# Two transformer blocks on one core: the three products of branches and output as seven quarter products each

## What is computed

```python
a = gmlp_spatial_gating(z_u, z_v, gmlp_ln_g[i], gmlp_ln_b[i], gmlp_w_s[i], gmlp_b_s[i])
b = forgetting_attention(q, k, v, f_logit, b_f[i])
y_a = jnp.einsum('bsc,cd->bsd', a, w_branch_a[i])
y_b = jnp.einsum('bsc,cd->bsd', b, w_branch_b[i])
merged = gate_a * y_a + gate_b * y_b
x = x + jnp.einsum('bsd,de->bse', merged, w_out[i])
h2 = rmsnorm_2(x, norm_ffn_g[i])
up = jnp.einsum('bsd,df->bsf', h2, w_up[i])
```

## Time and profile before

| | us |
|---|---|
| median of 3 runs (1606.82 to 1606.89) | 1606.87 |
| profiled execution, its own time | 1607.59 |
| its span on the core | 1605.9 |
| TensorE busy | 1587.6 (99%) |
| VectorE busy | 1078.5 (67%) |
| ScalarE busy | 710.6 (44%) |
| POOL busy | 181.5 (11%) |

### The profile page before, as it was taken

One profiled execution on the slowest core, in us unless ns is written; L12 is line 12 of the kernel. 1 busy time (PEld: TensorE's weight loads), 2 busy tenths in 40 slices (PEclk: granted clock), 3 DMA queues, 4 the chain that ended last, 5 costly groups with the idle time before them and its releaser, 6 DMA issues.

```text
span 1605.9 us, 20446 instructions
## 1 busy us (share of the span) xinstructions
PE 1587.6 (99%) x8187; PEld 1305.8 (81%) x8187; DVE 1078.5 (67%) x1494; ACT 710.6 (44%) x1018; POOL 181.5 (11%) x263
## 2 busy tenths in 40 slices
PE   9999999999999999999999999999999999999998
PEld 7877777888888888878788887888888888888888
DVE  6756788669393865657744477445566876878857
ACT  6524575545252524415662156342334443443544
POOL 0001055000000000024500255000000000000000
PEclk9999999999999999999999999999999999999999
DMA  5233321264757522331022211322237347344221
GB/s 191 80 106 125 123 95 53 79 210 131 236 132 235 131 106 94 116 138 72 27 105 83 101 53 53 136 101 105 93 143 262 102 135 238 93 154 158 105 106 53
DMA packets 32894, 195.14 MB, mean 122 GB/s; under 512 B 4320, under 2 KB 6816, under 8 KB 11296
## 3 DMA queue, kind: packets, MB, share of 16 engines
q1 hardware_dynamic: 25056, 160.20, 27.0%
q0 software_dynamic: 2880, 20.97, 6.8%
q10 hardware_dynamic: 4864, 12.66, 2.2%
HBM read 187.50 MB, written 6.32 MB: 121 GB/s over the span
## 4 chain that ended last, share of the span: by engine, by line
PE 87%; DVE 7%; issue 2%; ACT 2%; POOL 1%; DMA 0%; DVEq 0%; ACTq 0%; POOLq 0%
PE bank L767 20%; PE bank L769 19%; PE bank L768 19%; PE bank L1189 3%; PE bank L1190 3%; PE bank L1191 3%; PE bank L815 3%; PE bank L817 3%; PE bank L816 3%; PE bank L1000 1%; PE bank L775 1%; PE bank L985 1%; DVE w_lo L2370 1%; PE bank L744 1%; DVE up_c L2668 1%
## 5 line engine op out<-in xcount | busy, mean ns | idle before, releaser
L767 PE MATMUL bank<-a_hi,w_hi 128*128 128x512 f32 x1160 | 456.8, 394 | 0.6 <-DVE x L2030 0.6
L769 PE MATMUL bank<-a_hi,w_lo 128*128 128x512 f32 x1160 | 452.0, 390 | 0.0
L768 PE MATMUL bank<-a_lo,w_hi 128*128 128x512 f32 x1160 | 451.6, 389 | 0.0
L1375 ACT ACTIVATE w_hi<-w_raw 128x2048 fp32r<-128x2048 f32 x95 | 181.3, 1908 | 184.5 <-DMA w_raw<-in_strips 182.7
L769 PEld LDWEIGHTS bank<-a_hi,w_lo 128*128 128x128 f32 x1160 | 217.8, 188 | 45.9
L767 PEld LDWEIGHTS bank<-a_hi,w_hi 128*128 128x128 f32 x1160 | 217.9, 188 | 45.3 <-issue 2.3
L768 PEld LDWEIGHTS bank<-a_lo,w_hi 128*128 128x128 f32 x1160 | 218.0, 188 | 43.0 <-issue 0.2
L1951 DVE TENSOR_TENSOR w_lo<-w_raw,w_hi 128x2048 fp32r<-128x2048 f32 x92 | 210.9, 2293 | 54.4 <-ACT w_hi L1375 54.3
L1189 PE MATMUL bank<-w_hi,t_hi 128*128 128x512 f32 x280 | 109.3, 390 | 0.1
L1191 PE MATMUL bank<-w_hi,t_lo 128*128 128x512 f32 x280 | 109.0, 389 | 0.0
L1190 PE MATMUL bank<-w_lo,t_hi 128*128 128x512 f32 x280 | 109.0, 389 | 0.0
(11 more groups left out here) (364 smaller groups left out, 2658.0 us busy)
## 6 DMA issues: line engine op xcount, KB each, us to landing
w_raw<-in_strips SPq DMA_DIRECT2D x107, 1024.0 KB, 4.8
a_part<-in_parts SPq DMA_DIRECT2D x25, 1024.0 KB, 7.4
a_part<-in_parts POOLq DMA_DIRECT2D x20, 1024.0 KB, 9.1
spare<-in_parts SPq DMA_DIRECT2D x5, 1024.0 KB, 15.0
spare<-in_strips SPq DMA_DIRECT2D x5, 1024.0 KB, 4.9
seg_in<-cum_kept ACTq DMA_DIRECT2D x16, 256.0 KB, 3.5
x_kept<-x ACTq DMA_DIRECT2D x2, 2048.0 KB, 9.2
x<-x_kept SPq DMA_DIRECT2D x2, 2048.0 KB, 9.9
```

What stands on the lines that cost most here:

```text
L767: mm(ps[:, :], w_hi[slot][:, k, cols], hi[:, k, :], start=(k == 0), stop=False)
L768: mm(ps[:, :], w_hi[slot][:, k, cols], lo[:, k, :], start=False, stop=False)
L769: return mm(ps[:, :], w_lo[slot][:, k, cols], hi[:, k, :], start=False, stop=(k == kt - 1))
L1375: run(w_hi[j], w_raw[j], ACT.Copy).then_inc(hi_split, 1)
```

## The change

branch_b, branch_a and out2 are each computed as seven products of quarters. The weight (1024 x 1024) is cut in four quarters of 512 x 512, the operand in four of 512 features x 256 positions (`quad(buf, i, j)`: position half i, feature half j). Each product has one weight quarter or a sum of quarters as stationary operand, 48 matmuls of 256 columns into two banks, of which each holds two feature tiles. Products 2 and 3 add onto the banks of products 0 and 1, product 4 onto those of product 2.

- **Weights.** Four of the seven weights per matrix are sums (of 2, 2, 3 and 4 quarters). They are made in DRAM ahead of time: SP copies a quarter to `pre` behind each of twelve strip loads from ff2_3 on, and POOL issues twelve DMAs that add to them, six in attention 2a, one per head, and six during u and qk2b. In the new stages the strips are loaded to buffers of their own, two in turn (`fold_raw`, in the place of `x` for the branches, elsewhere for out2), each after VectorE has split the strip before the last.
- **Operands.** Four quarters (`high_four`, `low_four`: three plain, one a difference) and three further sums (`high_three`, `low_three`) per stage; VectorE makes the sums (`fold_sums`), partly over the operand itself. Those of branch_b are begun in gate_a, those of branch_a in branch_b, and those of out2 as soon as a quarter of `merged` is there.
- **Results.** ScalarE keeps the first two products' banks in SBUF (`keep_first`, `keep_second`), VectorE combines (`keep_sums`, `take_11`, `take_21`, `take_22`, `take_12`, `gate_part`, `add_known`). GpSimd does none of this work.
- **x** is read back in two halves in branch_a, with SP waiting for strips' splits, and the tiles' norm for up0 is done in two groups of four. The first weight parts of down0 are loaded after out2's last read of a bank.

The diff, cut to its core:

```diff
 PHASES += [(f"{w}{g}", 7 if f"{w}{g}" in SEVEN else 4) for g in range(FF_GROUPS) for w in ("ff1_", "ff2_")]
...
+FOLD_BANK = [6, 4, 6, 4, 6, 0, 2]
+FOLD_QUAD = [1, 0, 1, 2, 3, 0, 2]
+FOLD_FOUR = {0: 1, 1: 0, 3: 2, 4: 3}
+FOLD_THREE = {2: 0, 5: 1, 6: 2}
+THREE_QUAD = [(1, 0), (0, 0), (0, 1)]
+THREE_RAW = [(0, 0), (1, 0), (0, 1)]
+FOLD_SOURCE = [0, (0, 0), 2, (1, 0), 3, 1, (1, 1)]
+PRE_SUMS = [(0, 1), (0, 0), (0, 0), (1, 0)]
+PRE_COPIES = [(kind, f) for kind in range(4) for f in range(3)]
...
+                    sp_eng.wait_ge(dve_evac, EVAC0["out2"] + FILLS["out2"])
...
+                if s in FOLDED:
+                    n = s - FIRST[FOLD[0]]
+                    if n == 0:
+                        sp_eng.wait_ge(pv_done, 2 * 3 * HEADS8)
+                        sp_eng.wait_ge(summed, 16 * (12 + 4 * FF_SEVEN))
+                    elif n == 14:
+                        sp_eng.wait_ge(fold_step, FOLD_STEP0 + 5)
+                    elif n == 15:
+                        sp_eng.wait_ge(*low_ready(s - 3))
+                    elif n != 1:
+                        sp_eng.wait_ge(*low_ready(s - 2))
+                    f, i = FOLDED[s]
+                    source = FOLD_SOURCE[i]
+                    sp_eng.dma_start(flat(fold_at(s)), pre[source, f] if isinstance(source, int) else fold_part(f, source)).then_inc(fold_loaded[n % 3], 16)
+                    if n == 15:
+                        for h in range(2):
+                            sp_eng.wait_ge(*low_ready(s - 3 + h))
+                            half = slice(4 * h, 4 * h + 4)
+                            sp_eng.dma_start(x[:, half, :], x_kept[:, half, :]).then_inc(x_loaded[0], 16)
+                    continue
...
+                if 0 <= s - FIRST["ff2_3"] - 1 < len(PRE_COPIES):
+                    kind, f = PRE_COPIES[s - FIRST["ff2_3"] - 1]
+                    sp_eng.dma_start(pre[kind, f], fold_part(f, PRE_SUMS[kind])).then_inc(copied[kind // 2], 16)
...
-                if s == FIRST["gate_a"] + 3:
-                    sp_eng.wait_ge(pv_done, 2 * 3 * HEADS8)
-                    sp_eng.dma_start(x, x_kept).then_inc(x_loaded[0], 16)
...
+                    if call == "2a" and n % TT == 2 and 1 <= n // TT <= 6:
+                        add_part(*PRE_COPIES[n // TT - 1])
...
+            def add_part(kind, f):
+                if f == 0:
+                    pool.wait_ge(summed, 16 * (4 * FF_SEVEN + (0, 0, 6, 9)[kind]))
+                if f == 0 and kind in (0, 2):
+                    pool.wait_ge(copied[kind // 2], COPIED0[kind // 2] + 16 * 6)
+                other = (fold_part(f, (1, 1)), fold_part(f, (0, 1)), pre[0, f], pre[2, f])[kind]
+                pool.dma_start(pre[kind, f], other, accum_op=ALU.add, max_dma_last_dim=8192).then_inc(summed, 16)
...
+            for n, (kind, f) in enumerate(PRE_COPIES[6:]):
+                pool.wait_ge(unit_done, 2 * (FIRST["u"] + n + 1))
+                add_part(kind, f)
...
-            stream("branch_b", feature_k, B, ready=lambda k: pe.wait_ge(att_lo, 4 + k + 1))
-            stream("branch_a", feature_k, A, ready=wait_tiles(amix_lo))
-            stream("out2", feature_k, B, ready=wait_tiles(m_lo))
...
+            def folded(f):
+                for i in range(7):
+                    s = FIRST[FOLD[f]] + i
+                    slot, (t, k0) = s % W_SLOTS, QUADS[FOLD_QUAD[i]]
+                    hi, lo = quad(fold_hi[f], t, k0), quad(fold_lo[f], t, k0)
+                    pe.wait_ge(*low_ready(s))
+                    if i in FOLD_THREE:
+                        pe.wait_ge(three_lo, 3 * f + FOLD_THREE[i] + 1)
+                    else:
+                        pe.wait_ge(four_lo, 4 * f + FOLD_FOUR[i] + 1)
+                    for h in range(2):
+                        fold_bank(f, i, h)
+                        for e in range(2):
+                            ps = bank[FOLD_BANK[i] + h][:, e * (T // 2):(e + 1) * (T // 2)]
+                            cols = slice((2 * h + e) * P, (2 * h + e + 1) * P)
+                            for k in range(W4):
+                                mm(ps, w_hi4[slot][:, k, cols], hi[:, k, :], start=(e == 0 and k == 0 and i in (0, 1, 5, 6)), stop=False, skip_group_check=True)
+                                mm(ps, w_hi4[slot][:, k, cols], lo[:, k, :], start=False, stop=False, skip_group_check=True)
+                                last = mm(ps, w_lo4[slot][:, k, cols], hi[:, k, :], start=False, stop=(k == W4 - 1), skip_group_check=True)
+                        last.then_inc(unit_done, 1)
...
+            def high_strip(f, i):
+                s = FIRST[FOLD[f]] + i
+                act.wait_ge(fold_loaded[(s - FIRST[FOLD[0]]) % 3], fold_count(s))
+                act.wait_ge(unit_done, 2 * (s - W_SLOTS) + 2)
+                run(w_hi[s % W_SLOTS], fold_at(s), ACT.Copy).then_inc(hi_split, 1)
...
+            def high_three(f, n):
+                act.wait_ge(fold_sum, FOLD_SUM0 + 4 * f + (3, 2, 4)[n])
+                act.wait_ge(unit_done, 2 * (FIRST[FOLD[f]] + (0, 1, 3)[n]) + 2)
+                run(quad(fold_hi[f], *THREE_QUAD[n]), quad(fold_src[f], *THREE_RAW[n]), ACT.Copy).then_inc(three_hi, 1)
...
+                    act.wait_ge(unit_done, 2 * FIRST[FOLD[f]] + h + 1)
+                    run(fold_q[f][h], halves(6 + h), ACT.Copy).then_inc(snapped, 1)
...
+            sigmoids("gate_a", gate_t, 6, KT)
+            load_sqrt()
+            high_strip(0, 2)
+            high_four(1, 0)
+            high_four(1, 1)
+            keep_first(0)
+            high_three(0, 0)
+            high_strip(0, 3)
...
+            high_three(2, 2)
+            hi(FIRST["up0"])
...
+            def keep_sums(f):
+                src, e0 = fold_src[f], EVAC0[FOLD[f]]
+                dve.wait_ge(fold_sum, FOLD_SUM0 + 4 * f + 4)
+                for h in range(2):
+                    product_ready(f, 2, h)
+                    dve.wait_ge(snapped, SNAPPED0 + 4 * f + 2 + h + 1)
+                    v.tensor_tensor(quad(src, 0, 0, h), halves(6 + h), quad(fold_kept[f], 1, 1, h), ALU.add).then_inc(dve_evac, 1)
+                if f == 2:
+                    for h in range(2):
+                        dve.wait_ge(dve_evac, e0 + h + 1)
+                        fold_do(v.tensor_tensor(fold_q[f][h], quad(src, 0, 0, h), fold_q[f][h], ALU.subtract))
...
+            def gate_part(f, i, j, ready):
+                new, gate, total = quad(fold_src[f], 1, 0), quad(gate3, i, j), quad(merged3, i, j)
+                if f == 0:
+                    fold_do(v.tensor_tensor(total, total, new, ALU.mult))
+                else:
+                    fold_do(v.tensor_tensor(new, new, gate, ALU.mult))
+                    v.tensor_tensor(total, total, new, ALU.add).then_inc(merged_ready, 1)
+                    dve.wait_ge(merged_ready, ready)
...
             for j in range(KT):
                 scaled_evac("gate_a", j, gate_t[:, j * T:(j + 1) * T])
-                split_attention(j)
-                if j % 2:
+                if j in (1, 3):
                     lo(FIRST["gate_a"] + j // 2 + 2)
-            def low_a(g):
-                dve.wait_ge(amix_hi, g + 1)
-                v.tensor_tensor(a_lo[:, g, :], u_t[:, g * T:(g + 1) * T], a_hi[:, g, :].bitcast(F32), ALU.subtract).then_inc(amix_lo, 1)
-            for j in range(KT):
-                mt = merged[:, j * T:(j + 1) * T]
-                dve.wait_ge(unit_done, 2 * FIRST["branch_b"] + j + 1)
-                dve.wait_ge(gated, j + 1)
-                v.tensor_tensor(mt, mt, bank[j % 4][:, :], ALU.mult).then_inc(dve_evac, 1)
-                low_a(j)
-                if j % 2:
-                    lo(FIRST["branch_b"] + j // 2 + 2)
-            for j in range(KT):
-                gt, mt = gate_t[:, j * T:(j + 1) * T], merged[:, j * T:(j + 1) * T]
-                dve.wait_ge(unit_done, 2 * FIRST["branch_a"] + j + 1)
-                dve.wait_ge(gated, KT + j + 1)
-                v.tensor_tensor(gt, gt, bank[j % 4][:, :], ALU.mult).then_inc(dve_evac, 1)
-                dve.wait_ge(dve_evac, EVAC0["branch_a"] + j + 1)
-                v.tensor_tensor(mt, mt, gt, ALU.add).then_inc(merged_ready, 1)
-                dve.wait_ge(m_hi, j + 1)
-                v.tensor_tensor(b_lo[:, j, :], mt, b_hi[:, j, :].bitcast(F32), ALU.subtract).then_inc(m_lo, 1)
-                if j % 2:
-                    lo(FIRST["branch_a"] + j // 2 + 2)
-            dve.wait_ge(x_loaded[0], 48)
-            for m in range(KT):
-                add_x("out2", m, m)
+                if 1 <= j <= 4:
+                    low_four(0, j - 1)
+                if j in (4, 6):
+                    low_strip(0, j // 2 - 2)
+                if j in (0, 3, 5, 7):
+                    fold_sums(0, (0, 3, 5, 7).index(j))
+            low_four(1, 0)
+            fold_sums(1, 0)
+            low_strip(0, 2)
+            low_four(1, 1)
+            fold_sums(1, 1)
+            low_three(0, 0)
+            low_strip(0, 3)
+            fold_sums(1, 2)
+            low_three(0, 1)
```

(39 more changed lines are left out.)

322 lines of the change are left out of this document (276 added, 46 removed).

## The result

| | before | changed |
|---|---|---|
| median of 5 runs, us | 1606.87 | 1614.28 |
| lowest to highest, us | 1606.80 to 1608.07 | 1614.08 to 1616.50 |
| profiled execution, own time / span, us | 1607.59 / 1605.9 | 1614.08 / 1612.3 |

The changed kernel takes 1.0047 times as long as the one before, 95% interval 1.0033 to 1.0061: 7.4 us more, where I forecast 4.3. The median grows by 7.4, the profiled execution by 6.5 and its span by 6.4; what follows accounts for the 6.4. One of run clock's five executions took 1746.21 us at a granted clock of 0.851 and is left out of its interval; its other four took 1611.84 to 1614.19.

The account below looks back on a forecast made before the run. TensorE's matmuls were taken to bound the three stages, with new waits from the order of VectorE's list. 1606.87 + 3.8 (path to up0's third unit) + 0.5 (elsewhere) = 1611.2 us; range 1602.5 to 1617.0.

Parts of the forecast that it names:

- Matmuls, -9.6: branch_b, branch_a, out2: 21 products of 48 256-column matmuls at 0.120 us take 121.0 us instead of 130.6.
- Places 1 and 2: TensorE waits for VectorE's operand splits before product 2 of branch_b (2.6 us) and product 2 of out2 (3.5 us).
- Place 3: Start of up0: its first pair ends 4.6 us late, then TensorE waits 3.0 us before the summing matmuls.
- my walk: Engine lists followed from branch_b's first matmul to up0's third unit: 145.7 us against 141.9, so +3.8, the value taken.
- the sum of the path: From branch_b into up0, matmul saving plus the waits: -9.6 + 2.6 + 3.5 + 4.6 + 3.0 = +4.1 us.
- the clock falls: Rival: idling brings TensorE to 1.2 GHz for one product, up to 5.8 us more, 1613 to 1617; chance 0.04.
- slow landings: Rival: strip loads land in 7.4 us instead of 4.8, delaying out2 and up0, about 1616 us; chance 0.12.
- a longer attention 2a: Rival: attention 2a loses more than 0.5 us, 1613 to 1616; chance 0.06.
- Elsewhere, 0.5: Six adding DMAs on POOL in attention 2a cost +0.5 us (0 to 5.2); other adding DMAs, copies and strip loads 0.
- Full gain: Rival: TensorE sets the pace throughout and all 9.6 us stay, 1597.2 us; chance 0.08.
- hidden tail: Rival: x, norm and first split hide behind up0's first pair, so 3.6 us stay, 1603.3 us; chance 0.10.

Follow-up runs that it names:

- clock: Changed kernel with filling matmuls on TensorE in the idle times before product 2 of out2 and before up0's first pair; 1613.47 us.
- place1: Changed kernel with VectorE's and ScalarE's lists reordered so product 2 of branch_b's strip split and operand precede branch_a's second operand quarter; 1612.15 us.
- place2: Changed kernel with take_12(1) put behind low_strip(2,2) and low_three(2,0) in VectorE's list; 1612.53 us.
- bank: Changed kernel with take_22(2) alone put ahead of the splits of up0's first four operand tiles; 1613.72 us.
- clock2: Changed kernel with the edits of place1 and clock together; 1609.82 us.
- sums: Kernel before with only the weight sums added (12 DRAM copies, 12 adding DMAs), their results unused; 1607.71 us.
- tail: Changed kernel with add_known(1,1), add_known(0,1) and take_22(2) put ahead of the split of up0's first strip in VectorE's list; 1610.45 us.
- adds: Kernel of stat with all twelve adding DMAs issued beside u and qk2b, none in attention 2a; 1603.45 us.
- stat: Changed kernel with the reorderings of place1, place2 and tail, and the summing matmuls moved into up0's third unit; 1603.96 us.

## Why the prediction was right and where it was wrong

**Matmuls, -9.6: right.** In the new stages they start 0.120 us apart at 2.4 GHz. With 17 of them at 0.21, 21 products took 1.5 us more than 121.0.

**Places 1 and 2, 2.6 and 3.5: right.** Measured from start to start and less the 0.12 of a matmul, 2.4 and 3.3. VectorE's wait for branch_a's first quarter ended 5.85 us behind branch_b's first matmul, where I had 5.88. place1 and place2 show that the order of VectorE's list makes them.

**Place 3, 4.6 and 3.0: right in sum, wrong in its mechanism.** I let the pair go tile by tile, with the first at 128.2. It waits in one piece, 5.8 us, because the stream waits for banks 0 and 1 ahead of its first tile, and VectorE's reads of them stand behind three of up0's tiles. The 134.2 and the 10.9 us of a pair give 145.1, just where my walk had the sum of squares ready; since the products ended 1.3 us later than forecast, that is partly luck. What sets the third unit is the sum: in run bank the pair starts 2.0 us earlier and TensorE waits for the sum instead. In sum, with the clock at 1.00 (clock2), out2's end to third unit takes 7.3 us more than before, where I had 7.6. The late start thus costs little by itself; it turns waits that would be spread into one long idle time. The 3.0 was 2.7 by my own figures (142.5 to 145.2), which is why the sum of the path gave 4.1 and the walk 3.8.

**The clock: the term that the sum lacked.** The step that failed is the rival "the clock falls", put at 0.04 because all stretches of work in the kernel before have 1.00. That was no evidence: in these stages the kernel before never idles. The changed one does, and the clock fell behind two of its three idle times. In the profile it costs 1.5 us in out2 and 1.0 us in up0's pair (2.4 us of slow matmuls, the rest lies beside VectorE's sum of squares): 3.8 + 1.5 + 1.0 = 6.3 against 6.1 measured. Removed together in clock2: 2.5 us at the third unit, 2.3 in the median. The median of 1614.28 lies beyond the 2.7 us that I gave the forecast on each side, and inside the price of this rival (1613 to 1617). The range held it only because it also had room for slow landings and a longer attention 2a, which did not come: that part is luck.

The Trainium skill, page "TensorE: Matmul & The Clock Gate", section "HAM oscillation", warns of just this, idle gaps between bursts. I cited it and gave it one sentence. The runs bear it out behind each of eight idle times of 3.2 us and more, and show the fall behind shorter ones too, in some executions and not in others.

**Elsewhere, 0.5: right.** 0.4 in this profile; 0.3 alone in sums, not clear of nothing; 0.2 to 0.7 by the length of attention 2a. Where the clock fell there it was up to 1.6, within the 0 to 5.2 given but not by the mechanism that I gave for it. Copies and strip loads cost nothing that shows, the latter land as forecast (the page of the changed kernel, part 6):

```profile
fold_raw<-pre SPq DMA_DIRECT2D x12, 1024.0 KB, 4.8
fold_raw<-in_parts SPq DMA_DIRECT2D x9, 1024.0 KB, 4.8
```

**The rivals.** Full gain and hidden tail did not come; slow landings neither, with 4.8 us in both rows of fold_raw.

## What to carry over

Seven products instead of eight pay only if the other engines' lists are laid out for it: 1614.3 with the change as it stands; 1603.5 with the same arithmetic, lists reordered at three places, and the summing matmuls and adding DMAs moved; 1606.9 before. When an estimate creates idle time on TensorE in one piece, add the price of matmuls at 1.2 GHz behind it (here 1.5 us for 256 columns, up to 2.4 for 512), in full behind 3.2 us and more of idle time and as a chance behind some 2 us, as the runs here had it, and look at every wait that gathers small ones into one, such as a wait for all banks ahead of the first tile. Idle time of another engine that a repair is to use may be gone once the earlier repairs are in.

## What the runs showed of the hardware

- The lower clock does not come with every idle time of the same length. Behind the 2.3 us of idle time of place 1 it came in three of five profiles (clock, place2, bank; not in the changed kernel or tail), behind the 1.9 us ahead of up0 in one of two (adds, not stat), behind the 1.9 us ahead of tail's summing matmuls in the one there is. Behind each unfilled one of 3.2 us and more it came, eight times in five profiles (changed, place1, place2, tail, bank). And it came in attention 2a in four of nine profiles, where no single idle time just before was longer than 1.25 us (adds). Each time in the three stages and up0 some 3 to 5 us of work ran at a granted clock near 0.5, then 1.00 again.
- Single executions of one kernel differ the same way. Of clock2's eleven, the two with a mean granted clock of 1.000 took 1608.41 and 1608.63 us, the six with 0.998 took 1609.82 to 1610.48.
- Filling matmuls into a bank that nobody reads kept the clock at 1.00 over 5.6 us without useful work (clock2), at no cost in the end time.
- The two halves of such a trade can hide each other in a median: the profiles of stat and adds differ by 1.4 us up to branch_b, most of it one fall of the clock, and, the other way, by 8 slow matmuls.
